# Pre-norm deferred to the input projections' evictions, with x and the index projection first, in a two-layer hybrid attention trunk

## The reference

```python
h = _rmsnorm(x, pre_norm_g[i])           # x * rsqrt(mean(x*x) + eps) * g
z = h @ w_in[i]
qa, ka, va, qi, ki, wi, ga, qb, kb, vb, gb = _split_in(z)
...
y = jnp.concatenate([oa * silu(ga), ob * silu(gb)], axis=-1) @ w_out[i]
x = x + _rmsnorm(y, post_norm_g[i])
gate = jax.nn.sigmoid(x @ w_ple_gate[i])
e = (p[i] @ w_ple_proj[i]) * gate
x = x + _rmsnorm(e, ple_norm_g[i])
```

## Time and profile before

| | us |
|---|---|
| median of three runs | 375.98 |
| the profiled execution's own time | 376.63 |
| its span | 374.8 |
| busy: TensorE (PE) | 362.0 (97%) |
| busy: VectorE (DVE) | 261.2 (70%) |
| busy: ScalarE (ACT) | 223.0 (59%) |
| busy: GpSimd (POOL) | 66.7 (18%) |
| idle of TensorE before a product, for w_lo | 3.4 |
| mean share of the 16 DMA engines, head (0 to 40 us) | 0.90 |
| the same, 40 to 120 us | 0.58 |

### The profile page before, as it was taken

One profiled execution on the slowest core, in us unless ns is written; L12 is line 12 of the kernel. 1 busy time (PEld: TensorE's weight loads), 2 busy tenths in 40 slices (PEclk: granted clock), 3 DMA queues, 4 the chain that ended last, 5 costly groups with the idle time before them and its releaser, 6 DMA issues.

```text
span 374.8 us, 5604 instructions
## 1 busy us (share of the span) xinstructions
PE 362.0 (97%) x1932; PEld 300.6 (80%) x1932; DVE 261.2 (70%) x450; ACT 223.0 (59%) x451; POOL 66.7 (18%) x122
## 2 busy tenths in 40 slices
PE   7798999999999999999999999999999999999992
PEld 7596788788877888888889878788887788888881
DVE  2654977889873676587697478788986467558643
ACT  4655674775875753554684548577586575366221
POOL 1514513032500000004005512104150000000000
PEclk9899999999999999999999999999999999999999
DMA  7998846465564354567754845546457335551011
GB/s 251 319 183 312 290 141 186 114 174 162 165 194 149 113 170 143 184 201 146 201 164 150 267 126 157 168 120 207 124 168 226 112 114 168 171 176 47 2 41 71
DMA packets 32075, 61.64 MB, mean 164 GB/s; under 512 B 2384, under 2 KB 4688, under 8 KB 32048
## 3 DMA queue, kind: packets, MB, share of 16 engines
q1 hardware_dynamic: 30928, 58.01, 49.8%
q0 software_dynamic: 1120, 3.28, 4.6%
HBM read 60.23 MB, written 1.05 MB: 163 GB/s over the span
## 4 chain that ended last, share of the span: by engine, by line
PE 88%; DMA 6%; issue 2%; DVE 2%; ACT 1%; SPq 0%; DVEq 0%; POOLq 0%; POOL 0%
PE proj L951 25%; PE proj L953 24%; PE proj L952 23%; PE pv L1091 4%; DMA raw<-in_w_in_dram 3%; PE sc L1063 3%; PE sc L993 3%; DMA g_norm<-in_pre_norm_g_dram 2%; PE tr L1076 2%; PE tr L1009 2%; PE sc L1047 1%; PE sc L1023 1%; DVE w_lo L708 1%; DVE work L739 0%; ACT w_hi L522 0%
## 5 line engine op out<-in xcount | busy, mean ns | idle before, releaser
L951 PE MATMUL proj<-w_hi,act_hi 128*128 128x512 f32 (+1 forms) x416 | 166.4, 400 | 1.3 <-DVE w_lo L708 1.1
L953 PE MATMUL proj<-w_hi,act_lo 128*128 128x512 f32 (+1 forms) x416 | 160.1, 385 | 0.0
L952 PE MATMUL proj<-w_lo,act_hi 128*128 128x512 f32 (+1 forms) x416 | 159.9, 384 | 0.0
L708 DVE TENSOR_TENSOR w_lo<-raw,w_hi 128x1024 fp32r<-128x1024 f32 (+1 forms) x108 | 128.0, 1203 | 17.7 <-ACT w_hi L522 16.9
L522 ACT ACTIVATE w_hi<-raw 128x1024 fp32r<-128x1024 f32 (+1 forms) x108 | 109.9, 1041 | 6.9 <-DMA raw<-in_w_in_dram 4.9
L951 PEld LDWEIGHTS proj<-w_hi,act_hi 128*128 128x128 f32 x416 | 78.2, 188 | 17.3 <-DVE w_lo L708 1.3
L953 PEld LDWEIGHTS proj<-w_hi,act_lo 128*128 128x128 f32 x416 | 78.1, 188 | 16.0
L952 PEld LDWEIGHTS proj<-w_lo,act_hi 128*128 128x128 f32 x416 | 78.3, 188 | 12.8
L470 POOL TENSOR_TENSOR rstd<-var,minus_half 128x1 f32<-128x1 f32 x12 | 6.7, 554 | 192.2 <-DVE var L698 177.0
L625 ACT ACTIVATE probs<-sc,neg_max 128x128 f32<-128x128 f32 (+1 forms) x64 | 26.0, 429 | 13.4 <-DVE neg_max L796 13.4
L522 ACT ACTIVATE act_hi<-sc 128x512 fp32r<-128x512 f32 x24 | 13.6, 597 | 32.7 <-PE sc L993 32.7
(11 more groups left out here) (124 smaller groups left out, 368.6 us busy)
## 6 DMA issues: line engine op xcount, KB each, us to landing
raw<-in_w_in_dram SPq DMA_DIRECT2D x64, 512.0 KB, 4.1
raw<-in_w_out_dram SPq DMA_DIRECT2D x16, 512.0 KB, 3.4
raw<-in_w_ple_gate_dram SPq DMA_DIRECT2D x16, 512.0 KB, 4.1
raw<-in_w_in_dram SPq DMA_DIRECT2D x8, 324.0 KB, 7.2
raw<-in_w_ple_proj_dram SPq DMA_DIRECT2D x4, 512.0 KB, 3.4
resid<-in_x_dram SPq DMA_DIRECT2D x2, 512.0 KB, 7.5
g_norm<-in_post_norm_g_dram POOLq DMA_DIRECT2D x2, 512.0 KB, 5.6
g_ple<-in_ple_norm_g_dram POOLq DMA_DIRECT2D x2, 512.0 KB, 7.5
```

The lines of the kernel that those rows point to most:

```text
L708: nc.vector.tensor_tensor(w_lo[:, g % SLOTS, 0:nk * cols], raw[:, g % RAW_SLOTS, 0:nk * cols], w_hi[:, g % SLOTS, 0:nk * cols].bitcast(fp3 ...
L951: nc.tensor.matmul(ps, src_hi[:, b, k0 + k, :], hi, start=(first_u and k == 0), stop=False)
L952: nc.tensor.matmul(ps, src_hi[:, b, k0 + k, :], lo, start=False, stop=False)
L953: last = nc.tensor.matmul(ps, src_lo[:, b, k0 + k, :], hi, start=False, stop=last_k)
```

## The change

The gain g is no longer multiplied into x before the transpose, nor is rstd. The transposes of t8 take x (resid) itself; each slice of 128 of the model width then lies on the partitions, so its gain is one number per partition (g_col, all gains of both layers, loaded as 16 rows of 128 and transposed once, step "gT"). act_hi is copied with that scale, in four copies of 128 columns, and act_lo is made by four scaled subtractions. rstd, one number per row, is multiplied in where the projections are evicted (a scale per partition), and in the gate's product. "pre" keeps the square, the sum, var and the power, and loses the product. The indexer's weights lose their factor 1/2, which goes into the relu's scale.

The order changes too. In layer 0 x comes first, in four half-blocks, then IDX's weights; p and PLE's weights follow, and IDX stands ahead of PLE. The warming multiplications are 4, 2 and 6, the latter two behind the first two t8. In layer 1 t8 of h for block 0 stands right behind WG, then IDX of block 0, and the last "ple0" follows the t8. All of QB comes after this head; in layer 1 half of it stood inside. TI, D and the numbers of PLACE are set anew against it. The broadcast loads of the pre-norm's gain are gone, those of the post-norm's and embedding norm's gains are issued by GpSimd in the middle of the layer (behind PV 2), and the small loads behind pT.

```diff
-UNITS = [("PLE", n, 0, KU, N) for n in range(2)]
+UNITS = []
 for _c in IN_CHUNKS:
+    if _c == "QB":
+        UNITS += [("PLE", n, 0, KU, N) for n in range(2)]
...
-B0_ORDER = [("PLE", 0), ("PLE", 1)] + [(c, 0) for c in IN_CHUNKS] + [("WO", 0), ("WO", 1), ("WG", 0), ("WG", 1)]
+B0_ORDER = [("IDX", 0), ("PLE", 0), ("PLE", 1)] + [(c, 0) for c in IN_CHUNKS[1:]] + [("WO", 0), ("WO", 1), ("WG", 0), ("WG", 1)]
...
-WARM = 4, 8
+WARM = 4, 2, 6
...
-    TI=0,
-    D=3,
...
+    TI=[1, 6],
+    D=[2, 11],
...
+    pre0=[0, 0],
+    h0=[1, 1],
+    p0=4,
+    psq=0,
+    ple1=2,
+    pre1=5,
+    h1=[3, 4],
+    START=[3, 4, 7, 7, 9, 13, 15, 16, 17, 17])
...
+    ple = [(n, b) for b in range(NB) for n in range(2)]
     t8 = lambda src, b: [("t8", src, b, 0), ("t8", src, b, 1)]
     y8 = lambda b, half: [("t8", "y", b, half)]
     if L == 0:
-        out += [("pT", 0), ("pre", 0, 0)]
-        mms("PLE", ple, {0: [("pre", 1, 0)], 2: t8("h", 0), 3: t8("h", 1)})
-        mms("IDX", both, {})
-        mms("QB", both, {3: [("TI", 0)], 5: [("D", 0)]})
+        out += [("gT",)] + t8("h", 0)
+        head = one(0) + one(1) + [(UQ + n, b) for n, b in ple]
+        side = [(i, ("pre", b, 0)) for b, i in enumerate(PLACE["pre0"])]
+        side += [(i, ("t8", "h", 1, half)) for half, i in enumerate(PLACE["h0"])] + [(PLACE["p0"], ("pT", 0))]
     else:
-        out += [("ple0", 1, 1, L - 1)]
-        mms("PLE", ple, {0: t8("h", 0) + [("psq", 1, 1, L - 1), ("ple1", 1, L - 1)], 2: [("pre", 1, L)]})
-        mms("IDX", one(0), {})
-        mms("QB", one(0), {1: t8("h", 1)})
-        mms("IDX", one(1), {})
-        mms("QB", one(1), {1: [("TI", 0)], 3: [("D", 0)]})
-
-    mid = [[] for _ in range(7 * len(both))]
-    placed = [(PLACE["TI"], ("TI", 1)), (PLACE["D"], ("D", 1)), (PLACE["lam"], ("lam",))]
+        out += t8("h", 0) + [("ple0", 1, 1, L - 1)]
+        head = one(0) + [(UQ + n, b) for n, b in ple[:2]] + one(1) + [(UQ + n, b) for n, b in ple[2:]]
+        side = [(PLACE["psq"], ("psq", 1, 1, L - 1)), (PLACE["ple1"], ("ple1", 1, L - 1)), (PLACE["pre1"], ("pre", 1, L))]
+        side += [(i, ("t8", "h", 1, half)) for half, i in enumerate(PLACE["h1"])]
+    mms("IDX", head, {i: [step for at, step in side if at == i] for i in range(len(head))})
...
+            load_x(0, 0)
+            sp.dma_start(g_rows[:, :], pre_norm_g.rearrange("l (k p) -> (l k) p", p=P)).then_inc(gpre_in, 16)
+            load_x(0, 1)
...
+                if g == 1:
+                    load_x(1, 0)
+                    load_x(1, 1)
+                elif g == 3:
+                    sp.dma_start(p_raw[:, :, :], p[0, 0].rearrange("(b p) d -> p b d", p=P)).then_inc(p_in[0], 16)
+                elif g == 4:
...
+                if kind == "pT" and s[1] + 1 < DEPTH:
+                    pool.wait_ge(ptr_done, s[1] + 1)
+                    load_p(s[1] + 1)
+                if kind == "pT" and s[1] == 0:
+                    load_small(0)
+                if kind == "PV" and s[1] == 2:
+                    if L > 0:
+                        pool.wait_ge(wo_scaled, L * 4)
...
-                    pool.dma_start(g_norm[:, :], bcast(pre_norm_g[L + 1, :])).then_inc(gpre_in[L + 1], 16)
...
-                        copy(z_idx[:, b, 0:nqk], ps[:, 0:nqk])
-                        copy(z_idx[:, b, nqk:nqk + HEAD], ps[:, 4 * HEAD:nqk])
-                        copy(w_idx[:, b, :], ps[:, nqk:nqk + IDX_HEADS], IDX_HEADS ** -0.5).then_inc(idx_out, 1)
+                        act.wait_ge(rstd_done[0], L * 2 + b + 1)
+                        copy(z_idx[:, b, 0:nqk], ps[:, 0:nqk], rstd[:, 0, b:b + 1])
+                        copy(z_idx[:, b, nqk:nqk + HEAD], ps[:, 4 * HEAD:nqk], rstd[:, 0, b:b + 1])
+                        copy(w_idx[:, b, :], ps[:, nqk:nqk + IDX_HEADS], rstd[:, 0, b:b + 1]).then_inc(idx_out, 1)
...
+                        copy(z_view(chunk, b), ps[:, :], rstd[:, 0, b:b + 1]).then_inc(z_out, 1)
...
+                elif kind == "gT":
+                    act.wait_ge(gcol_tr, 1)
+                    copy(g_col[:, :], tr[:, 0:DEPTH * KT]).then_inc(gcol_done, 1)
...
+                        act.wait_ge(gcol_done, 1)
+                        for j in range(4):
+                            k = 4 * s[3] + j
+                            last = copy(act_hi[:, s[2], k, :], sc[i % 2][:, j * P:(j + 1) * P],
+                                        g_col[:, L * KT + k:L * KT + k + 1])
+                        last.then_inc(at_hi, 1)
...
+                                             scale=(HEAD * IDX_HEADS) ** -0.5)\
...
+                    nc.vector.scalar_tensor_tensor(gate[:, b, :], proj[bank_of(chunk, n, b)][:, :],
+                                                   rstd[:, 0, b:b + 1], gate[:, b, :], ALU.mult, ALU.mult)\
...
-                    dve.wait_ge(rstd_done[0], M * 2 + b + 1)
-                    dve.wait_ge(gpre_in[M], 16)
-                    nc.vector.scalar_tensor_tensor(work[:, b, :], resid[:, b, :], rstd[:, 0, b:b + 1], g_norm[:, :],
-                                                   ALU.mult, ALU.mult).then_inc(h_done, 1)
...
+                            ins = nc.vector.scalar_tensor_tensor(
+                                act_lo[:, s[2], k, :], sc[i % 2][:, j * P:(j + 1) * P],
+                                g_col[:, L * KT + k:L * KT + k + 1], act_hi[:, s[2], k, :].bitcast(fp32), ALU.mult,
+                                ALU.subtract)
...
-                if chunk == "PLE":
+                if chunk == "IDX":
                     if L > 0:
-                        pe.wait_ge(wg_sig, prev * 4 + (1 if n == 0 else 3) + b)
-                elif chunk == "IDX":
-                    pe.wait_ge(ple_out, L * 4 + 2 + b + 1)
+                        pe.wait_ge(wg_sig, prev * 4 + 2 + b + 1)
+                elif chunk == "PLE" and n == 0:
+                    if L > 0:
+                        pe.wait_ge(wg_sig, prev * 4 + b + 1)
+                elif chunk == "PLE":
+                    pe.wait_ge(idx_out, L * 2 + b + 1)
                 elif chunk == "QB":
-                    pe.wait_ge(ple_out, L * 4 + b + 1)
+                    pe.wait_ge(ple_out, L * 4 + 2 * b + 1)
                 elif chunk == "KB":
-                    pe.wait_ge(idx_out, L * 2 + b + 1)
+                    pe.wait_ge(ple_out, L * 4 + 2 * b + 2)
...
+                    pe.wait_ge(gpre_in, 16)
+                    nc.tensor.transpose(tr[:, 0:DEPTH * KT], g_rows[:, :], ident[0:DEPTH * KT, 0:DEPTH * KT])\
+                        .then_inc(gcol_tr, 1)
...
-                        pe.wait_ge(h_done, L * 2 + b + 1)
+                    if src == "h" and L == 0:
+                        pe.wait_ge(x_in[b][half], 16)
+                    elif src == "h":
+                        pe.wait_ge(x2_done, (L - 1) * 4 + 2 * b + half + 1)
...
+                    for w in range(WARM[1 + half] if L + b == 0 and src == "h" else 0):
+                        nc.tensor.matmul(pv[:, 0:P], ident[:, :], ident[:, :], start=True, stop=True)
```

99 lines of the change are left out of this document (46 added, 53 removed).

## The result

The changed kernel takes 377.02 us in the median (375.63 to 378.83, 17 runs) against 375.22 for the kernel before, measured beside it (373.95 to 377.2, 17 runs): ratio 1.0047, 95% interval [1.0031, 1.0063], 1.8 us slower. The forecast said 375.1, faster; its range of 373.0 to 378.0 holds the measured time only because the rivals that end slower had widened it. The profiled execution of the changed kernel has a span of 375.6 and its own time is 377.41; before, 374.8.

A forecast was written before the change was run, and what follows sets the result against it. TensorE's product stream, 97% busy, was taken as the bound, its start set by early waits for w_lo. Head gain 3.6 less boundary loss 2.75 gives 0.85 off 376.63; less 0.65 to the median, 375.1 us, range 373.0 to 378.0.

The forecast's parts named there:

- the rivals that end slower: Clock halved across both boundary waits, 378.2 us, chance 0.12; QB's last weights landing late, 377.6 us after 9 us, chance 0.12.
- the head's gain: Start of the program: the third QB piece comes at 30.55 instead of 34.17, a gain of 3.6 us.
- lies 0.65 above the median: The profiled execution of the kernel before, 376.63 us, was taken as 0.65 above the runs' median of 375.98.
- First wait: Layer boundary: TensorE waits 2.2 us for act_lo of block 0's transposes of h, before IDX.
- The second: Layer boundary: block 1's transposes wait 0.55 us for the embedding norm's last sum.
- Whole loss: Layer boundary: the two TensorE waits together lose 2.75 us, with bounds of 1.2 to 3.3.
- Four scaled copies and products: Split act_hi priced at 1.15 us on ScalarE and act_lo at 1.13 on VectorE, against 0.60 and 0.69 whole.
- The wait of 2.7: The boundary's first wait by the skill page's price of 0.41 us per scaled copy; the total would be 0.5 worse.
- Rival A with one fall: Layer boundary: the clock falls once behind the hole, 1.55 us more, 376.7 us in all; chance 0.14.
- Rival C: Slow small loads delay QB's last weights: landing after 9 us costs 2.5, giving 377.6; after 12.8, 6.3; chance 0.12.
- is only moved and is left out: Head: D for block 0 now stands ahead of the third QB piece; its products were not counted in the walk.
- Rival B: Split copies cost what whole ones do: boundary waits 1.2 and 0.3, head 0.6 earlier, 373.3 us; chance 0.20.

## Why the prediction was wrong

**Two steps failed: the head's gain was sized against one execution, and the clock fall at the boundary stood at nothing in the sum.** "A gain of 3.6" was right for the execution it was worked from: 165.74 - 161.95 is 3.79 where D did not wait. But 2.31 of it was a hole of 2.31, which was 1.50 in the next profile, and the 0.50 clock behind it. Against the second profile of the kernel before the head gains 1.48; against a usual execution about 2.4 (3.79 less the 1.41 by which the first profiled execution lay over the median of 17), an estimate. The forecast took 0.65 off for the slow execution ("lies 0.65 above the median") and also kept the gain that came from ending its misfortune, which counts it twice.

The account on one base, the first profiled execution of the kernel before (376.63), against the second of the changed one (377.25, the median of its twelve):

| us | forecast | measured |
|---|---|---|
| head | -3.60 | -3.79 |
| boundary, even clock | +2.75 | +3.06 |
| clock fall behind the boundary's hole | 0 | +1.36 |
| taken off to reach the median | -0.65 | 0 |
| sum | -1.50 | +0.63 |

The clock is the largest line of the miss. Either step alone turns the sign of the forecast change of 0.85 gained: with the clock's 1.36 it is 0.51 lost, with 1.48 in place of 3.6 for the head 1.27 lost, with 2.4 still 0.35 lost.

**The boundary: right in mechanism, a little small.** First wait forecast 2.2, which the profile lists as 2.05 in both profiles of the changed kernel; counted as the forecast counted it, from where the next product would start behind the transposes (188.92 + 0.79 = 189.71) to where it does (192.01), it is 2.30. The second was forecast as 0.55 and is 0.39 in the same count (0.23 as listed). Whole loss forecast 2.75, measured 3.06 by the marks; the 0.4 beyond the two waits was not taken apart. Four scaled copies and products, forecast at 1.15 and 1.13, took 1.15 and 1.13. The wait of 2.7 that I worked out by the Trainium skill (ScalarE: Activation LUTs, Rules for kernel authors) was too high: eight scaled copies took 2.18, 0.27 each.

**Rival A with one fall was the case that came.** It had 0.14 and gave 376.7 at a cost of 1.55; the second profile shows the fall, at 1.36, and nine of twelve executions carry its mean clock. The argument against it was that TensorE is warm and streams ahead of the hole. It streamed for 150 us ahead of it, and the clock fell nevertheless. The Trainium skill's page (TensorE: Matmul & The Clock Gate, HAM oscillation) describes such a fall for a kernel that waits for data behind every short burst of products, with waits longer than the holes here; that one hole in a full stream does it is what these runs add. I had it in a rival, not in the sum. That the fall did not happen in the first profile of the changed kernel, with the same 2.05, makes it a chance per execution: a price times a share, by what is known now 1.36 x 9/12 = 1.0, would have been the honest term. That A's 376.7 lies near 377.02 is in part luck: without the 0.65 that was counted twice it would have been 377.3.

**Rival C: right on the transfer, wrong on the weights it hits.** The late load was KB's first unit, not QB's last; it held ScalarE until 29.33 and with it the copy that D needs, 1.6. That D "is only moved and is left out" was the step that missed it: D had been put behind a ScalarE instruction that waits for a DMA. It is an event of some executions (one profile of the first two of the changed kernel), not a fixed cost.

**Rival B** assumed whole-copy prices: first wait 1.2, total 373.3. The kernel with whole copies measured 1.07 and 373.29. As a forecast of this change it was wrong. As arithmetic it held, its last digit by luck: against the first profiled execution that kernel gained 3.16 (4.52 in the head, less 1.36), not 2.7, and 0.18 was to be taken off for the median, not 0.65.

The account of the 1.8, from the two second profiles: head -1.48, boundary +3.06, clock +1.36, together 2.94, and their spans differ by 3.0. The medians differ by 1.8 to 2.0; the profiled execution of the kernel before was itself the fastest of its twelve, 0.63 under their median, and a quarter of the changed kernel's executions are without the fall, which explains most of the difference.

What stays open: which loads make KB's unit late. The small loads of lambda as its cause were not tried apart. Nor is it shown what makes the hole of the kernel before 2.31 in one execution and 1.50 in another, or how the executions of that kernel that were not profiled divide between the two.

## What to carry to other kernels

Take a gain that consists of ending a hole or a clock fall only if a second profile of the same kernel has it too, or if the run times do: one execution's misfortune is not the kernel's. Before moving independent work ahead or away, list what each block of it covered; here the embedding's four products were the only work at the boundary that did not need the transposes, and giving the layers two different orders kept the gain of one place without the loss of the other. A producer split into pieces should signal in pieces as well where its consumer waits for it (it gave 1.5 to 1.8 there and nothing where the wait was covered), and a hole near 2 us in a warm stream should be priced with the clock that may fall behind it.
